# Weight units that stream as the moving operand placed 32 bytes into their slot

## The chip, the cores and the metric

The kernel runs on one core of one Trainium2 chip. The metric is the device time of one execution in microseconds (us). The kernel before takes 2200.12 us, the median of 3 runs (2200.06 to 2201.48).

## What is computed

A small transformer in float32: 256 tokens of width 1024 pass through four layers. Layers 0 and 1 have grouped-query attention (in layer 1 with a sliding window) and layers 2 and 3 a gated delta rule beside dilated attention. The feed-forward part is dense in layers 0, 2 and 3; in layer 1 it is a mixture of 8 experts of which each token uses two:

```
q, k, v = project_qkv(x, w_qkv[i], cos, sin)                 # x @ w, 1024 -> 1536
x = layer_norm(alpha * x + a.reshape(...) @ w_o[i], ...)
swiglu:     (silu(x @ w_gate) * (x @ w_up)) @ w_down         # 1024 -> 3584 -> 1024
moe_swiglu: for e in range(8): out += gates[..., e] * swiglu(x, w_gate[e], w_up[e], w_down[e])
x = x + (p[i] @ w_ple_proj[i]) * sigmoid(x @ w_ple_gate[i])
```

Nearly all the work is activations times weight matrices, and every weight is used once: the weights are streamed from memory.

## The kernel before, in words

**Units.** All weights come as units of 1 MB, [128 partitions x 2048 columns] of float32 (8192 bytes in each partition). SyncE loads them, in the order in which they are used, into `raw`, a ring of 6 slots (L619 in the expert loop, L639 elsewhere). ScalarE copies a unit into a slot of `w_hi`, rounded to the type float32r (`split_hi`, L535), and VectorE writes what the rounding left, `raw - w_hi`, into the same slot of `w_lo` (`split_lo`, L540). `w_hi` and `w_lo` have SPLIT = 3 slots each, one behind another, and unit i lies in slot `place(i)`. The activations are split in the same way into two parts, `xT` and `aT_hi`/`aT_lo`.

**Products.** A product of activations and weights is three float32r matmuls (`mm3`, L829): high by high, high by low, low by high. `nc.tensor.matmul(out, stationary, moving)` first loads its stationary operand, here 128 columns, and then streams the moving one. Weights take one of two roles:

- as the **moving** operand, in pieces of 512 columns, with 128 columns of activations stationary: `part` (the projections qkv, o, the embedding gate, and units 6 to 13 of the input projection of layers 2 and 3), the dense `down`, and all of the experts' `gate_up` and `down`.
- as the **stationary** operand, in pieces of 128 columns, with 256 columns of activations moving: `features` (L897 and L899; the dense gate and up steps but the last two) and `features_in` (through L829; the last two steps, and units 0 to 5 of the input projection). L897 streams the high and the low part of the activations, 256 columns each, in one matmul.

Every piece starts at a multiple of 128 columns in its unit, and every slot and every tensor of activations starts at a multiple of 64 bytes in its partition. The router multiplies by a stationary operand of 8 columns only (`wr_hi`, `wr_lo`), through the same line L829.

**Order.** The order of all the work is written out by hand. Before TensorE reads a unit it waits for VectorE's mark on it (`unit`, L511). ScalarE may overwrite the slot of unit i - 3 with unit i once TensorE has read unit i - 3 for the last time, and SyncE may load unit i + 6 into `raw` once VectorE has split unit i. The experts run in a loop of 8 turns; each turn uses 42 units, 12 matmuls of 512 columns each, and a few transposes (L1160, L1188). A matmul of plain float32 of 512 columns (L816, L824, which keep the engine warm) stands in the trace as two MATMUL instructions.

Of the kernel before, what the change touches and what calls it, by code (L numbers as in the profile page):

```python
# [21 lines left out]
F32R = mybir.dt.float32r  # L22
F32 = mybir.dt.float32
I32 = mybir.dt.int32
ALU = mybir.AluOpType
# [3 lines left out]
P = 128  # L29
# [9 lines left out]
UNIT = 2048  # L39
WARM_START, WARM_LN, WARM_RMS = 4, 2, 4  # L40
RAW = 6
SPLIT = 3
# [188 lines left out]
def build_program(nc, A, plan, debug=None):  # L231
    cst_np, cst_at = constants()
    NC = cst_np.shape[1]
    with ExitStack() as ctx:
        def sb(name, shape, dt=F32):
            return ctx.enter_context(nc.sbuf_tensor(name, shape, dt))


        raw = sb("raw", [P, RAW, UNIT])
        w_hi = sb("w_hi", [P, SPLIT, UNIT], F32R)  # L240
        w_lo = sb("w_lo", [P, SPLIT, UNIT], F32R)
        cst = sb("cst", [P, NC])
        X = sb("X", [P, NT, DM])
        R = sb("R", [P, NT, DM])
# [128 lines left out]
        def events(tag):  # L373
            ev = Events(nc, ctx, plan, tag)

            class E:
                pass
            E.ev = ev
            E.groups = Groups(ev, "groups", 1)
            E.free = [Free(ev, f"free{b}", 1) for b in range(8)]  # L380
            E.dve = ev.new("dve_step")
            E.act = ev.new("act_step")
            E.loaded = [ev.new(f"loaded{s}", 16) for s in range(RAW)]
            E.hi = ev.new("hi_ready")
            E.lo = ev.new("lo_ready")
            E.put = ev.new("ye_stored", 16)
            return E
        M = events("")
# [86 lines left out]
        unit_at, n = {}, 0  # L475
# [9 lines left out]
        after = expert_base + NE * TURN  # L485

        def split_no(i):

            return i - sum(1 for w in whole if w < i)

        def place(i):
            return split_no(i) % SPLIT

        def key_of(i):

            if i >= after and i - after < SPLIT:
                return expert_base + TURN + i - after
            return i
# [8 lines left out]
        def index(key, base=None):  # L507
            return unit_at[key] if base is None else base + order.index(key)
        order = [k for k, _, _ in EXPERT]

        def unit(E, pe, key, base=None):  # L511

            i = index(key, base)
            pe.wait_ge(*E.lo.at("unit", key_of(i)))
            return w_hi[:, place(i), :], w_lo[:, place(i), :]

        def released(E, i, *key):

# [8 lines left out]
        def split_hi(E, ac, i):  # L527

            src = wait_loaded(E, ac, i)
            back = i - SPLIT - (1 if any(i - SPLIT <= w < i for w in whole) else 0)  # L530
            if E is V and i < SPLIT:
                ac.wait_ge(E.groups.sem, 1 + E.ev.turn * plan.per.get("ovf_groups", 0))
            elif back >= 0:
                ac.wait_ge(*reader(E, back))
            nc.scalar.copy(w_hi[:, place(i), :], src).then_inc(*E.hi.mark("unit", i))  # L535

        def split_lo(E, ve, i):

            ve.wait_ge(*E.hi.at("unit", i))
            nc.vector.tensor_tensor(w_lo[:, place(i), :], raw[:, i % RAW, :], w_hi[:, place(i), :].bitcast(F32), ALU.subtract) \  # L540
                .then_inc(*E.lo.mark("unit", i))

        def ahead(E, split, eng, key, base=None):
# [947 lines left out]
        def _(ac):  # L1491
# [3 lines left out]
            def walk(*key):  # L1495
                ahead(M, split_hi, ac, key)
# [390 lines left out]
            for L in range(2):  # L1887
                if L:
                    walk("pg", 0, 3)
                    copy_T((L, "in"), L, 1)  # L1890
                mixer(L)
                want_root()
                if L == 1:
                    ac.wait_ge(*params.at("wr"))
                    nc.scalar.copy(wr_s[0][:, :, :], wr[:, :, :]).then_inc(*M.act.mark("wr"))
                walk("wo", L, 0)
                walk("wo", L, 2)
                norm_root(L, "mix", 0)
                walk("wo", L, 1)
                norm_root(L, "mix", 1)  # L1900
                for t in range(NT):
                    copy_T((L, "mix"), L, t)
                walk("wo", L, 3)
                if L == 0:
                    dense_act(0)
                    want_root()
                    norm_root(L, "ffn", 0)
                    walk("dn", L, FFN_STEPS[L] - 2)
                    walk("dn", L, FFN_STEPS[L] - 1)
                    norm_root(L, "ffn", 1)  # L1910
                    copy_T((L, "ffn"), L, 0)
                    copy_T((L, "ffn"), L, 1)
                else:
                    for i in range(2):
                        split_hi(M, ac, expert_base + i)
                    ac.wait_ge(*M.groups.at("router"))
                    nc.scalar.copy(moe["lgT"][0:NE, :], bank[0][0:NE, 0:S]).then_inc(*M.free[0].mark("router"))
                    for t in range(NT):
                        ac.wait_ge(*x_ready.at(L, "mix", t))
                        ins = nc.scalar.activation(R[:, t, :], X[:, t, :], ACT.Copy, scale=ALPHA)  # L1920
                    ins.then_inc(*M.act.mark("scaled"))
                    ac.wait_ge(*decided.at("m"))
                    nc.scalar.activation(w2, w2, ACT.Exp).then_inc(*M.act.mark("w2"))
                    for i in range(2, SPLIT):
                        split_hi(M, ac, expert_base + i)
                    gathered(M, "moe", "first")
                    nc.scalar.preload_act_table(ACT.Silu)
                    with ac.Fori(0, NE) as e:
                        with ev.loop(e):
                            experts(M, "moe", expert_base)  # L1930
                    ac.wait_ge(*flag_done.at())
                    r = ac.value_load(flag_i[0:1, 0:1], min_val=0, max_val=1)
                    with ac.If(r > 0):
                        with ac.Fori(0, NE) as e:
                            with V.ev.loop(e):
                                experts(V, "ovf", 0)
                        ac.wait_ge(*V.groups.at("ovf", "dn", EXP_STEPS - 1))
                        for i in range(after, after + RAW):
                            ac.wait_ge(*V.loaded[i % RAW].at("again"))
                        for i in range(SPLIT):  # L1940
                            nc.scalar.copy(w_hi[:, place(after + i), :], raw[:, (after + i) % RAW, :]) \
                                .then_inc(*V.hi.mark("again", i))
                    want_root()
                    norm_root(L, "ffn", 0)
                    copy_T((L, "ffn"), L, 0)
                    norm_root(L, "ffn", 1)
                    copy_T((L, "ffn"), L, 1)

                def sigmoid(nb, t):
                    ac.wait_ge(*M.groups.at("pg", L, nb, t))  # L1950
                    nc.scalar.activation(att["sg"][:, 2 * nb + t, :], bank[2 * nb + t][:, :], ACT.Sigmoid) \
                        .then_inc(*M.free[2 * nb + t].mark("pg", L, nb, t))
                sigmoid(0, 0)
                walk("pg", L, 0)
                sigmoid(0, 1)
                walk("pg", L, 1)
                sigmoid(1, 0)
                if L == 0:
                    walk("pg", L, 2)
                    copy_T((1, "in"), 1, 0)  # L1960
                else:
                    want_root()
                    sum_squares(2, "in", 0, x_ready.at(1, "ple", 0))
                    nc.scalar.activation(spare, C("rms_eps"), ACT.Sigmoid)
                sigmoid(1, 1)
# [39 lines left out]
        def _(ve):  # L2005
            V_ = nc.vector
# [12 lines left out]
            def walk(*key):  # L2019
                ahead(M, split_lo, ve, key)  # L2020
# [620 lines left out]
            for L in range(2):  # L2641
# [39 lines left out]
                else:  # L2681
# [14 lines left out]
                    with ve.If(r > 0):  # L2696

                        for n, event in enumerate(V.free + [V.groups]):
                            V_.memset(tick[:, n:n + 1], 0.0).then_inc(event.sem, 1)
                        with ve.Fori(0, NE) as e:  # L2700
                            with V.ev.loop(e):
                                experts(V, "ovf", 0, e, 1)
                        for i in range(SPLIT):
                            u = after + i
                            ve.wait_ge(*V.hi.at("again", i))
                            V_.tensor_tensor(w_lo[:, place(u), :], raw[:, u % RAW, :], w_hi[:, place(u), :].bitcast(F32), ALU.subtract) \
                                .then_inc(*V.lo.mark("again", i))

                    def take_rows(t, nb, total):
# [181 lines left out]
```

## Time and profile before

| | |
|---|---|
| median of 3 runs | 2200.12 us |
| the profiled execution, its own time | 2201.47 us |
| its span, from the first instruction to the last | 2199.7 us |
| TensorE matmuls busy | 2164.4 us (98%), 11360 instructions |
| VectorE busy | 1724.8 us (78%) |
| ScalarE busy | 1416.0 us (64%) |
| mean granted TensorE clock | 0.999 of 2.4 GHz |
| read from memory | 564 MB |

"Busy" is the time in which at least one instruction of the engine was in flight. Matmuls overlap in the pipeline, so the mean duration of one says little about the rate; the rate is the distance between the starts of matmuls that follow one another, or the time of a run of them in the chain of waits divided by their number. The profile names only the tensors that an instruction reads and writes, not the addresses.

### The profile page before, as it was taken

To read this page: it belongs to the slowest core of one execution; us is meant where nothing else is said; L and a number is where in the kernel's file an instruction comes from. 1 tells how busy PE (TensorE), PEld (TensorE's weight loads), DVE (VectorE), ACT (ScalarE), POOL (GpSimd) and SP (SyncE) were. 2 spreads that over 40 slices of the span, in tenths; PEclk is the share of its full clock that TensorE was granted. 3 is DMA by queue.
4 is the path that set the end of the run, shared out by engine and by line. 5 is a ranking of instruction groups with operands and counts; after the bars stand their busy time and mean duration, and the time that the engine had idled before them with its cause. 6 is when DMAs were issued, how large, how long until landed. Compare 5 with 4: busy or idle time off the path is not lost.

```text
span 2199.7 us, 30807 instructions
## 1 busy us (share of the span) xinstructions
PE 2164.4 (98%) x11360; PEld 1806.4 (82%) x11360; DVE 1724.8 (78%) x1976; ACT 1416.0 (64%) x1582; POOL 61.7 (3%) x96
## 2 busy tenths in 40 slices
PE   8999999999999999999999999999999999999998
PEld 6788897778888888888888887779978898988888
DVE  6766556688898888888888889767668886776887
ACT  6644444767777777777777777656566556565554
POOL 3000000020000000000000003000000000000000
PEclk9999999999999999999999999999999999999999
DMA  9755554369999999999999999843135554224451
GB/s 390 273 185 190 192 190 175 120 256 397 358 397 368 390 374 384 378 382 380 371 388 376 389 365 403 323 177 130 68 145 190 184 200 148 86 106 157 188 189 61
DMA packets 83523, 573.26 MB, mean 261 GB/s; under 512 B 9744, under 2 KB 10368, under 8 KB 18224
## 3 DMA queue, kind: packets, MB, share of 16 engines
q1 hardware_dynamic: 77760, 545.29, 65.0%
q0 software_dynamic: 5376, 26.12, 3.2%
q8 instruction: 63, 1.03, 0.2%
q10 hardware_dynamic: 288, 0.52, 0.1%
q14 instruction: 36, 0.29, 0.0%
HBM read 564.03 MB, written 17.83 MB: 265 GB/s over the span
## 4 chain that ended last, share of the span: by engine, by line
PE 87%; DVE 6%; ACT 4%; issue 2%; DMA 1%; SPq 0%; POOL 0%; DVEq 0%; ACTq 0%; POOLq 0%
PE bank L829 64%; PE bank L897 10%; PE bank L899 5%; DVE w_lo L540 1%; ACT w_hi L535 1%; PE bank L1188 1%; DVE arena L2411 1%; PE bank L1316 1%; PE bank L1326 1%; ACT arena L1533 1%; DMA raw<-in_wu_qkv 1%; PE bank L952 0%; DVE arena L2091 0%; PE bank L944 0%; PE bank L798 0%
## 5 line engine op out<-in xcount | busy, mean ns | idle before, releaser
L540 DVE TENSOR_TENSOR w_lo<-raw,w_hi 128x2048 fp32r<-128x2048 f32 x505 | 1156.1, 2300 | 249.4 <-ACT w_hi L535 247.7
L535 ACT CAST w_hi<-raw 128x2048 fp32r<-128x2048 f32 x505 | 964.4, 1912 | 357.5 <-PE bank L829 275.1
L829 PE MATMUL bank<-w_hi,xT 128*128 128x512 f32 x2368 | 751.5, 392 | 6.4 <-DVE w_lo L540 3.3
L829 PEld LDWEIGHTS bank<-w_hi,xT 128*128 128x128 f32 x2368 | 444.6, 188 | 107.6 <-issue 7.0
L829 PE MATMUL bank<-w_lo,xT 128*128 128x512 f32 x1184 | 461.0, 389 | 0.0
L829 PE MATMUL bank<-w_hi,aT_hi 128*128 128x512 f32 x864 | 344.4, 399 | 1.0 <-DVE w_lo L540 1.0
L897 PE MATMUL bank<-xT,w_hi 128*128 128x512 f32 x960 | 339.9, 398 | 1.2 <-DVE xT L2035 0.6
L829 PE MATMUL bank<-w_hi,aT_lo 128*128 128x512 f32 x864 | 337.3, 390 | 0.0
L829 PE MATMUL bank<-w_lo,aT_hi 128*128 128x512 f32 x864 | 336.7, 390 | 0.0
L899 PE MATMUL bank<-xT,w_lo 128*128 128x256 f32 x960 | 269.3, 281 | 0.0
L829 PEld LDWEIGHTS bank<-w_lo,xT 128*128 128x128 f32 x1184 | 222.5, 188 | 44.7 <-issue 0.5
L897 PEld LDWEIGHTS bank<-xT,w_hi 128*128 128x128 f32 x960 | 180.3, 188 | 47.0 <-DVE xT L2035 1.4
L829 PEld LDWEIGHTS bank<-w_hi,aT_hi 128*128 128x128 f32 x864 | 162.3, 188 | 35.6 <-issue 4.0
L829 PEld LDWEIGHTS bank<-w_hi,aT_lo 128*128 128x128 f32 x864 | 162.1, 188 | 35.5
L829 PEld LDWEIGHTS bank<-w_lo,aT_hi 128*128 128x128 f32 x864 | 162.5, 188 | 30.8
L899 PEld LDWEIGHTS bank<-xT,w_lo 128*128 128x128 f32 x960 | 181.2, 189 | 0.9
L829 PE MATMUL bank<-xT,w_hi 128*128 128x256 f32 x768 | 139.0, 283 | 0.0
L829 PEld LDWEIGHTS bank<-xT,w_hi 128*128 128x128 f32 x768 | 120.0, 192 | 0.5
L829 PE MATMUL bank<-xT,w_lo 128*128 128x256 f32 x384 | 108.6, 283 | 0.0
L1688 ACT ACTIVATE arena<-arena,fcw 128x256 f32<-128x256 f32 x72 | 39.4, 595 | 71.4 <-DVE arena L2225 71.4
L829 PEld LDWEIGHTS bank<-xT,w_lo 128*128 128x128 f32 x384 | 73.7, 192 | 0.0
L1648 ACT COPY arena<-bank 128x256 f32<-128x256 f32 x120 | 38.4, 371 | 50.4 <-PE bank L899 50.4
(348 smaller groups left out, 1689.2 us busy)
## 6 DMA issues: line engine op xcount, KB each, us to landing
raw<-in_wu_eg SPq DMA_DIRECT2D x112, 1024.0 KB, 7.3
raw<-in_wu_eu SPq DMA_DIRECT2D x112, 1024.0 KB, 7.2
raw<-in_wu_ed SPq DMA_DIRECT2D x112, 1024.0 KB, 7.2
raw<-in_wu_up SPq DMA_DIRECT2D x44, 1024.0 KB, 4.8
raw<-in_wu_ffn_gu SPq DMA_DIRECT2D x28, 1024.0 KB, 4.8
raw<-in_wu_in SPq DMA_DIRECT2D x28, 1024.0 KB, 4.8
raw<-in_wu_down SPq DMA_DIRECT2D x22, 1024.0 KB, 4.8
raw<-in_wu_ffn_d SPq DMA_DIRECT2D x14, 1024.0 KB, 4.8
```

What stands on the lines that cost most here:

```text
L535: nc.scalar.copy(w_hi[:, place(i), :], src).then_inc(*E.hi.mark("unit", i))
L540: nc.vector.tensor_tensor(w_lo[:, place(i), :], raw[:, i % RAW, :], w_hi[:, place(i), :].bitcast(F32), ALU.subtract) \
L829: mm = nc.tensor.matmul(o, l[i], r[j], start=(first and n == 0), stop=(last and n == 2), skip_group_check=not lone)
L897: nc.tensor.matmul(both, u[0][:, c0:c0 + P], x_both[:, :, kc, :], start=(kc == 0), stop=False, skip_group_check=True)
L899: mm = nc.tensor.matmul(o[:, S:2 * S], u[1][:, c0:c0 + P], xT[0][:, kc, :], start=False, stop=(kc == KC - 1), skip_group_check=True)
L1188: mm = nc.tensor.transpose(o[:, c * P:(c + 1) * P], moe["h"][:, f % 2, c * P:(c + 1) * P], ident)
L1316: of_level(n, "X", t, t, lambda dst, i: nc.tensor.matmul(dst, dn["LT"][:, i, :], dn["D"][:, i, :], start=True, stop=True))
L1326: of_level(n, "D", t, 2 + t, lambda dst, i: nc.tensor.matmul(dst, dn["DT"][:, i, :], dn["Xl"][:, i, :], start=True, stop=True))
L1533: ins = nc.scalar.activation(att["pr"][:, i, e, cols], att["s"][:, i, e, cols], ACT.Exp, bias=nmax[:, i, e, q:q + 1], scale=-1.0, accum_ou ...
L1648: ins = nc.scalar.copy(ffn["cor"][:, half, m, :], bank[4 + 2 * half + m][:, S:2 * S])
L1688: ins = nc.scalar.activation(buf[:, s % 2, m, :], src, ACT.Identity, bias=fcw[:, c, 3:4], scale=fcw[:, c, 2:3])
L2411: ins = V_.scalar_tensor_tensor(dn["cv"][:, c, d:S], bank[b][:, m * S:m * S + S - d], cw[:, L - 2, c, tap:tap + 1], dn["cv"][:, c, d:S], A ...
```

## The change

Each slot of `w_hi` and `w_lo` becomes 32 columns (128 bytes) longer, 8320 bytes instead of 8192. A unit whose matmuls use it as the moving operand stands 8 columns (32 bytes) behind the start of its slot; a unit that is used as the stationary operand starts where the slot starts. ScalarE, VectorE and TensorE take the place from one new function, `split_at`. No instruction is added, removed or moved in any engine's order, no wait changes, and every instruction handles as many elements as before. The tensors that are allocated behind the two (`cst`, `X`, `R`, `xT`, `aT` and the rest) start 768 bytes later.

```diff
         raw = sb("raw", [P, RAW, UNIT])
-        w_hi = sb("w_hi", [P, SPLIT, UNIT], F32R)
-        w_lo = sb("w_lo", [P, SPLIT, UNIT], F32R)
+        MOVING_AT = 8
+        w_room = [sb(f"w_{part}", [P, SPLIT, UNIT + 32], F32R) for part in ("hi", "lo")]
+        w_hi, w_lo = [w[:, :, MOVING_AT:MOVING_AT + UNIT] for w in w_room]
...
+        stationary = {i for key, i in unit_at.items() if (key[0] == "gu" or (key[0] == "in" and key[2] < 6))}
+
+        def split_at(E, i):
+
+            at = 0 if E is M and i in stationary else MOVING_AT
+            return [w[:, place(i), at:at + UNIT] for w in w_room]
...
             pe.wait_ge(*E.lo.at("unit", key_of(i)))
-            return w_hi[:, place(i), :], w_lo[:, place(i), :]
+            return split_at(E, i)
...
-            nc.scalar.copy(w_hi[:, place(i), :], src).then_inc(*E.hi.mark("unit", i))
+            nc.scalar.copy(split_at(E, i)[0], src).then_inc(*E.hi.mark("unit", i))
...
-            nc.vector.tensor_tensor(w_lo[:, place(i), :], raw[:, i % RAW, :], w_hi[:, place(i), :].bitcast(F32), ALU.subtract) \
+            hi, lo = split_at(E, i)
+            nc.vector.tensor_tensor(lo, raw[:, i % RAW, :], hi.bitcast(F32), ALU.subtract) \
```

The expert units are not in `unit_at`, so they all count as moving. The two other places that split units (for an overflow of the experts, a branch that this input does not take) are changed alike.

## Rows read from the trace of the kernel before

**Rows 1.** The page: busy time by engine, then the chain by engine and line.
```profile
PE 2164.4 (98%) x11360; PEld 1806.4 (82%) x11360; DVE 1724.8 (78%) x1976; ACT 1416.0 (64%) x1582; POOL 61.7 (3%) x96
...
PE 87%; DVE 6%; ACT 4%; issue 2%; DMA 1%; SPq 0%; POOL 0%; DVEq 0%; ACTq 0%; POOLq 0%
```

**Rows 2.** Groups of TensorE's instructions by shape; xcount, busy and mean, idle before.
```profile
L829 PE MATMUL bank<-w_hi,xT 128*128 128x512 f32 x2368 | 751.5, 392 | 6.4 <-DVE w_lo L540 3.3 <-DVE w_lo L2604 2.1 <-DVE xT L2035 0.7
L829 PE MATMUL bank<-w_lo,xT 128*128 128x512 f32 x1184 | 461.0, 389 | 0.0
L829 PE MATMUL bank<-w_hi,aT_hi 128*128 128x512 f32 x864 | 344.4, 399 | 1.0 <-DVE w_lo L540 1.0
...
L829 PE MATMUL bank<-w_hi,aT_lo 128*128 128x512 f32 x864 | 337.3, 390 | 0.0
L829 PE MATMUL bank<-w_lo,aT_hi 128*128 128x512 f32 x864 | 336.7, 390 | 0.0
```

**Rows 3.** Chain of waits, 600 to 700 us: start, length in us, what.
```profile
619.35 16.35 PE bank L829 x72
```

**Rows 4.** Timeline of TensorE, 296 to 302 us: weights stationary, 256 columns moving.
```profile
296.23 0.28 PE L829 MATMUL bank<-xT,w_lo 128*128 128x256 f32 x1
...
299.11 0.28 PE L829 MATMUL bank<-xT,w_lo 128*128 128x256 f32 x1
```

**Rows 5.** Timeline of TensorE, 452 to 455.6 us: the router, 8 stationary columns.
```profile
452.65 0.40 PE L829 MATMUL bank<-xT,wr_hi 128*8 128x256 f32 x2 [0.47 <-DVE xT L2032]
...
455.10 0.40 PE L829 MATMUL bank<-xT,wr_hi 128*8 128x256 f32 x2
```

**Rows 6.** Timeline of TensorE, 2001.5 to 2006 us: matmuls of plain float32.
```profile
2001.89 3.60 PE L816 MATMUL bank<-cst 128*128 128x512 f32 x8
2005.33 0.93 PE L798 MATMUL bank<-R,X 128*128 128x128 f32 x6
```

**Rows 7.** Chain of waits, 200 to 240 us: gate and up of the dense layer.
```profile
209.66 0.23 PE bank L897
...
220.61 5.50 PE bank L829 x24
```

**Rows 8.** Timeline of TensorE, 237 to 239 us: from gate and up to down.
```profile
237.24 0.40 PE L829 MATMUL bank<-w_hi,aT_hi 128*128 128x512 f32 x1
...
238.87 0.39 PE L829 MATMUL bank<-w_lo,aT_hi 128*128 128x512 f32 x1
```

**Rows 9.** Busy time in the expert loop: us, engines with counts, PEclk, DMA share, GB/s.
```profile
505.00:1435.00 930.00, 924.04 (x4182) 758.42 (x4180) 817.79 (x460) 689.76 (x470) 19.26 (x8) 1.00 0.97 377
```

**Rows 10.** Waits by total, 520 to 1400 us.
```profile
ACT w_hi L535 <- PE bank L829: 176.7, 252, 2.2
DVE w_lo L540 <- ACT w_hi L535: 100.9, 190, 1.5
```

**Rows 11.** DMA, 600 to 1300 us: GB/s in 40 slices; one unit's landing.
```profile
GB/s 406 414 366 382 370 361 350 424 404 370 368 361 385 358 411 383 389 367 379 355 394 384 402 372 382 371 352 405 381 400 387 367 375 338 415 400 378 386 362 363
...
raw<-in_wu_eg SPq DMA_DIRECT2D x82, 1024.0 KB, 7.3
```

**Rows 12.** Groups of ScalarE and VectorE by shape.
```profile
L535 ACT CAST w_hi<-raw 128x2048 fp32r<-128x2048 f32 x505 | 964.4, 1912 | 357.5 <-PE bank L829 275.1 <-PE bank L899 80.1 <-DMA raw<-in_wu_qkv 2.0
...
L540 DVE TENSOR_TENSOR w_lo<-raw,w_hi 128x2048 fp32r<-128x2048 f32 x505 | 1156.1, 2300 | 249.4 <-ACT w_hi L535 247.7
...
L2264 DVE SCALAR_TENSOR_TENSOR arena<-arena,fcw 128x255 f32<-128x255 f32 x72 | 31.7, 481 | 44.3 <-ACT arena L1688 44.3
...
L2159 DVE SCALAR_TENSOR_TENSOR X<-R,small,vec 128x1024 f32<-128x1024 f32 x8 | 10.3, 1285 | 0.3
```

More of the change, by code:

```diff
@@ L1940, in _ @@
                         for i in range(SPLIT):
-                            nc.scalar.copy(w_hi[:, place(after + i), :], raw[:, (after + i) % RAW, :]) \
+                            nc.scalar.copy(split_at(M, after + i)[0], raw[:, (after + i) % RAW, :]) \
                                 .then_inc(*V.hi.mark("again", i))
@@ L2705, in _ @@
                             ve.wait_ge(*V.hi.at("again", i))
-                            V_.tensor_tensor(w_lo[:, place(u), :], raw[:, u % RAW, :], w_hi[:, place(u), :].bitcast(F32), ALU.subtract) \
+                            hi, lo = split_at(M, u)
+                            V_.tensor_tensor(lo, raw[:, u % RAW, :], hi.bitcast(F32), ALU.subtract) \
                                 .then_inc(*V.lo.mark("again", i))
```

## The prediction, made before the changed kernel had run

> **What bounds the kernel now.** I read the page first. TensorE is busy for 2164.4 of 2199.7 us, and 87% of the chain that ended last is its own matmuls [rows 1]. The groups by shape say which: 2368 + 1184 + 3 x 864 = 6144 matmuls of 512 columns stream weights, and before the largest group the engine sat idle for only 6.4 us in the whole run [rows 2]. So TensorE seldom waits for a unit, and the question is its rate. The mean durations (389 to 399 ns) are those of a pipeline; the chain of waits gives the rate: a run of 72 such matmuls takes 16.35 us, 227.1 ns each [rows 3]. The granted clock there is 1.00 of 2.4 GHz [rows 9], at which 512 columns at one per cycle are 213.3 ns. Each matmul costs 13.8 ns more than its columns.
>
> I then looked for what that excess depends on.
> - Weights stationary, 256 columns moving: from 296.23 to 299.11 us stand eight groups of three, so 24 starts in 2.88 us, 120.0 ns each [rows 4]. 256 columns are 106.7 ns: excess 13.3 ns, the same for half the columns. It is a price per matmul, not per byte.
> - The router, only 8 stationary columns: seven groups of three from 452.65 to 455.10 us, 116.7 ns each [rows 5]. Excess 10.0 ns. With almost nothing to load into the array 3.3 ns go, 10 stay.
> - Plain float32: 8 instructions from 2001.89 to 2005.33 us, 430 ns each [rows 6]. That is two cycles per column (426.7 ns) and an excess of 3.3 ns, with the same load of 128 columns. The moving operand is read at half the rate there.
> - Gate and up, where one matmul streams two runs of 256 columns and the next one run: 31 pairs from 209.66 to 220.61 us, 353.2 ns a pair [rows 7]. Less 120.0 for the single run, the one with two runs takes 233.2 ns, 6.1 more than one run of 512.
> - Just behind such pairs the same down matmuls that later run at 227.1 start 1.63 us / 7 = 232.9 ns apart [rows 8]. So the excess is not a constant of the instruction: it depends on how the streams stood to one another before.
>
> My reading: when float32r is streamed at a column per cycle, reading the moving operand and loading the next stationary operand get in one another's way a little, and the phase between them matters. In the kernel before every operand of both kinds starts at a multiple of 64 bytes, so the trace shows a single setting of that phase. The change gives it another one, for 6144 of the matmuls.
>
> **The change, part by part.** *TensorE, weights moving.* 6144 matmuls, at an unknown change of price. From below, the most that can go is the excess down to that of plain float32, 13.8 - 3.3 = 10.5 ns: 6144 x 10.5 = 64.5 us. From above, the worst rate in these rows is that of a stream that starts a second run, +6.1 ns: 6144 x 6.1 = 37.5 us lost. Zero lies between. I take the nearest row in which the load is practically absent and all else is as before, the router's: 120.0 - 116.7 = 3.3 ns off each, 6144 x 3.3 = 20.3 us. That is the part of the excess which two streams out of each other's way would save; the other 10 ns stay in a row without a load, and nothing shows that an offset moves them.
>
> *TensorE, weights stationary.* These units keep their place and the activations that they meet stay at multiples of 64 bytes; only distances of 128 bytes and more change between tensors. I count 0, with 3.3 ns on some of them either way as the bound: the two shapes of L897 and L899 alone are 1920 matmuls, 6 us.
>
> *ScalarE and VectorE.* They write and read 32 bytes further on. 505 casts of 1912 ns and 505 subtractions of 2300 ns [rows 12]. The convolution (L2264) works on 255 columns that start one element into a row: 481 ns; the aligned L2159 takes 1285 ns for 1024 columns. At 1.042 ns a column that leaves 215 and 218 ns fixed: an odd start costs VectorE nothing visible. I count 0 for both. Even 50 ns on each would be covered: ScalarE waits 176.7 us and VectorE 100.9 us for others in the expert loop [rows 10].
>
> *What the gain triggers.* A unit is 12 matmuls, 2.73 us; a slot must be refilled within two units, 5.45 us, and needs 1.91 + 2.30 = 4.2 us. With 3.3 ns off each the window is 5.37 us, with 10.5 off 5.20: still enough. VectorE is busy for 817.8 of 930 us there (88%) [rows 9]; at the full gain that becomes 92%. The DMA moves 377 GB/s [rows 9]; the full gain asks for 377 x 227.1 / 216.6 = 395, and slices of the same stretch reach 424 [rows 11]. A transfer lands 7.3 us after its issue, out of six units, 16.4 us, less the 4.2 of the split. So neither takes the gain away, and as the runs of matmuls are themselves the path, all of it counts.
>
> *Sum.* The profiled execution's own time is 2201.5 us; less 20.3 is 2181.2. The median of the runs lies 1.3 us lower, so the forecast is 2179.8, say 2180 us.
>
> **What the pages say.** Two rules of the Trainium skill speak against this. "SBUF — State Buffer", section "Specifications (TRN2)", has lines of 16 bytes as the unit in which an operand is read; 32 bytes are two such lines, the operand starts on a line as before and touches as many, and by that rule the time stays at 2200. No row here can show it, as nothing of float32r starts elsewhere than at a multiple of 64 bytes. And "TensorE: Matmul & The Clock Gate", section "Step-by-step: what each phase is for", gives the moving operand and the weight load ports of their own, so that a load steals nothing from a running matmul. By that rule too nothing would change; the router's row disagrees in part, with 3.3 ns less when the load is small.
>
> **The rivals.**
> - *Nothing changes: 2200 us.* The excess is a fixed price of a float32r matmul. For it: it is 13.8 and 13.3 ns for 512 and 256 columns, as a fixed price would be, and the router's smaller one may come from the shorter load itself. In the kernel `turn_probs` transposes stationary data that start at odd elements, beside aligned transposes elsewhere, and nothing in TensorE's groups sets them apart. Against it: rows 8, where the same matmul has two prices.
> - *The whole excess goes.* The offset lets the two reads alternate without a meeting, and what is left is plain float32's 3.3 ns: 2200 - 64.5 = 2136 us. For it: that row has the same load. Against it: the router keeps 10 ns without one.
> - *Slower, on the far side of zero.* A run of 2048 bytes that begins 32 bytes into a 64-byte stretch ends in one more such stretch (33 instead of 32). If the reader fetches in stretches of 64 bytes, each matmul pays for a start in mid-stretch as L897 pays for its second run, 6.1 ns: 2200 + 37.5 = 2238 us. It decides from the first nanosecond, since nothing hides TensorE. For it: rows 7, a second start does cost. Against it: L897's second run lies 8 KB away, not next door.
> - *The change does less than it says.* All units of the experts and of `part` go through `split_at`, so 6144 matmuls are reached; I see no way in which only some would be.
>
> **How the numbers follow.** Forecast (a few ns off each moving matmul) 0.38; whole excess 0.15; nothing 0.26; slower 0.21. A measurement of this kernel tells a change from none at about 0.2%, 4.4 us. Faster 0.53, same 0.26, slower 0.21. The forecast's own range is 1.5 to 7 ns, 2157 to 2191 us. For 8 in 10 the range needs no change (2200), most of the whole excess (down to 2135) and the milder half of the slower case (up to 3 ns, 2219): 2135 to 2219 us.
>
> **What would show it right or wrong.** Right: in the expert loop a run of 72 matmuls in the chain takes 16.35 - 72 x 0.0033 = 16.11 us; the loop is shorter by 4032 x 3.3 ns = 13 us; the pairs of L897 and L899 stay at 353 ns and the 256-column matmuls with stationary weights at 120; L535 and L540 keep 1912 and 2300 ns. If the run takes 15.6 us the whole excess went; if 16.35, nothing; if about 16.8, the offset costs a start. The forecast's mechanism would be wrong if the stationary matmuls move as much as the moving ones, or if ScalarE's or VectorE's durations carry the difference, or if TensorE begins to wait for L540 in the expert loop by more than a few us.

## The result, and the profile after

The changed kernel takes 2229.41 us (median of 4 runs, 2229.19 to 2229.84), beside 2200.3 us for the kernel before (4 runs, 2200.06 to 2201.48). The ratio is 1.0129, with a 95% interval of 1.0116 to 1.0143: 29 us slower, where 20 us faster was forecast. 2229 also lies above the range of 2135 to 2219 us.

The page, line 1 and the first line of the chain, to be read beside [rows 1]:

```profile
PE 2195.4 (99%) x11360; PEld 1807.6 (81%) x11360; DVE 1726.1 (77%) x1976; ACT 1413.6 (63%) x1582; POOL 63.5 (3%) x96
...
PE 91%; DVE 4%; ACT 2%; issue 1%; DMA 1%; SPq 0%; POOL 0%; DVEq 0%; ACTq 0%; POOLq 0%
```

TensorE is busy 31.0 us longer in a span that is 28.3 us longer (2228.0 against 2199.7 us). VectorE's and ScalarE's busy time moved by 1.3 and 2.4 us. So the time went into TensorE's own work, and the next view shows into which instructions. These are its groups by shape (count, busy us, mean ns, idle before), beside [rows 2]; all lines of the kernel now stand 8 lower, L829 is L837, L897 and L899 are L905 and L907:

```profile
L837 PE MATMUL bank<-w_hi,xT 128*128 128x512 f32 x2368 | 762.9, 397 | 4.4 <-DVE w_lo L548 3.4 <-DVE xT L2043 0.7
L837 PE MATMUL bank<-w_lo,xT 128*128 128x512 f32 x1184 | 467.8, 395 | 0.0
L837 PE MATMUL bank<-w_hi,aT_hi 128*128 128x512 f32 x864 | 346.8, 401 | 1.0 <-DVE w_lo L548 1.0
L837 PE MATMUL bank<-w_hi,aT_lo 128*128 128x512 f32 x864 | 342.4, 396 | 0.0
L837 PE MATMUL bank<-w_lo,aT_hi 128*128 128x512 f32 x864 | 340.9, 395 | 0.0
L905 PE MATMUL bank<-xT,w_hi 128*128 128x512 f32 x960 | 338.7, 395 | 1.1 <-DVE xT L2043 0.6 <-issue 0.4
L907 PE MATMUL bank<-xT,w_lo 128*128 128x256 f32 x960 | 269.3, 281 | 0.0
```

The five groups with weights moving, 6144 matmuls, were busy for 2230.9 us and are now busy for 2260.8: +29.9, the whole loss. (Matmuls of different groups overlap in the pipeline, so these sums are larger than the engine's busy time.) The two groups with weights stationary, 339.9 and 269.3 us before, are at 338.7 and 269.3. Idle time in front of the first group fell, from 6.4 to 4.4 us: nobody waits more. (The distances from each start to the next, summed over the trace, give the same picture: +28.9 us for the five groups, -1.3 us for the pairs.)

The chain of waits in the expert loop (start, length in us, what), beside the 16.35 us of [rows 3]:

```profile
624.33 0.44 PE bank L1196 x4
624.77 16.79 PE bank L837 x72
641.56 0.44 PE bank L1196 x4
641.99 16.78 PE bank L837 x72
```

16.79 us are 233.2 ns each instead of 227.1. The transposes between two runs keep their 0.44 us. It holds for every run: of 30 such runs between 520 and 1430 us one takes 17.05 us and 29 take 16.78 or 16.79; in the kernel before one took 16.63 and 28 of 29 took 16.35. One turn of the loop was 118.65 us and is 121.42, which is 2.77 us for 504 matmuls, 5.5 ns each, and 22 us for eight turns. The other 7 us come from the 2112 moving matmuls outside it, where a run of 24 went from the 5.50 us of [rows 7] to 5.61 us.

A closer look at the steady part of one run, in the timeline of TensorE (start, length; the xN at the end of a line tells how many are grouped). The kernel before:

```profile
629.64 0.39 PE L829 MATMUL bank<-w_lo,xT 128*128 128x512 f32 x1
629.87 0.62 PE L829 MATMUL bank<-w_hi,xT 128*128 128x512 f32 x2
...
634.40 0.39 PE L829 MATMUL bank<-w_lo,xT 128*128 128x512 f32 x1
```

and the changed one:

```profile
634.64 0.40 PE L837 MATMUL bank<-w_lo,xT 128*128 128x512 f32 x1
634.87 0.63 PE L837 MATMUL bank<-w_hi,xT 128*128 128x512 f32 x2
...
639.53 0.40 PE L837 MATMUL bank<-w_lo,xT 128*128 128x512 f32 x1
```

Seven groups of three lie between first and last: 21 starts in 4.76 us, 226.7 ns each, before; 21 in 4.89 us, 232.9 ns each, after. At the full clock of 2.4 GHz 226.67 ns are 544 cycles and 233.33 ns are 560. The kernel before needs some eight to ten matmuls behind every interruption, of 224 to 236 ns each, until it runs at 544; that is [rows 8], seen from nearer. The changed kernel never gets there. So it loses 6.2 ns only on the matmuls behind this run-in, and 4.7 ns on the average over all 6144.

What could have carried the loss instead, and doesn't: the granted clock in the loop (the third number from the end), 1.00 as in [rows 9]:

```profile
505.00:1450.00 945.00, 940.47 (x4168) 757.37 (x4168) 815.70 (x449) 686.96 (x466) 21.19 (x8) 1.00 0.96 369
```

the waits of the two splits by total (us, times, longest), beside [rows 10]:

```profile
ACT w_hi L542 <- PE bank L837: 190.9, 247, 2.1
DVE w_lo L548 <- ACT w_hi L542: 115.9, 191, 1.5
```

and the splits themselves, ScalarE's and VectorE's groups by shape beside [rows 12]:

```profile
L542 ACT CAST w_hi<-raw 128x2048 fp32r<-128x2048 f32 x505 | 961.9, 1907 | 380.7 <-PE bank L837 296.9 <-PE bank L907 81.2 <-DMA raw<-in_wu_qkv 2.6
```

```profile
L548 DVE TENSOR_TENSOR w_lo<-raw,w_hi 128x2048 fp32r<-128x2048 f32 x505 | 1157.4, 2300 | 273.4 <-ACT w_hi L542 271.6
```

The casts take 1907 ns (1912 before), the subtractions 2300 as before, 32 bytes further on. ScalarE waits longer for TensorE, and VectorE for ScalarE; TensorE doesn't wait longer for them. The memory traffic fell from 377 to 369 GB/s, which is what the longer turn alone gives (377 x 118.65 / 121.42 = 368).

### The profile page after: what moved, and what is told of

It reads as the page before. It is cut to its first block, busy times and chain, and to the rows that moved or that the text cites. A ratio compares the mean times of both kernels' runs of the same rounds, so it can differ in the third digit from the quotient of the medians.

```text
span 2228.0 us, 30807 instructions
## 1 busy us (share of the span) xinstructions
PE 2195.4 (99%) x11360; PEld 1807.6 (81%) x11360; DVE 1726.1 (77%) x1976; ACT 1413.6 (63%) x1582; POOL 63.5 (3%) x96
## 4 chain that ended last, share of the span: by engine, by line
PE 91%; DVE 4%; ACT 2%; issue 1%; DMA 1%; SPq 0%; POOL 0%; DVEq 0%; ACTq 0%; POOLq 0%
PE bank L837 67%; PE bank L905 10%; PE bank L907 5%; PE bank L1196 1%; DVE w_lo L548 1%; PE bank L1324 1%; PE bank L1334 1%; ACT arena L1541 1%; DMA raw<-in_wu_qkv 1%; DVE arena L2099 0%; PE bank L960 0%; ACT w_hi L542 0%; DVE arena L2419 0%; PE bank L952 0%; PE bank L806 0%
## 5 line engine op out<-in xcount | busy, mean ns | idle before, releaser
L542 ACT CAST w_hi<-raw 128x2048 fp32r<-128x2048 f32 x505 | 961.9, 1907 | 380.7 <-PE bank L837 296.9
L837 PE MATMUL bank<-w_hi,xT 128*128 128x512 f32 x2368 | 762.9, 397 | 4.4 <-DVE w_lo L548 3.4
L837 PEld LDWEIGHTS bank<-w_hi,xT 128*128 128x128 f32 x2368 | 444.4, 188 | 115.6 <-DVE w_lo L548 5.4
L837 PE MATMUL bank<-w_lo,xT 128*128 128x512 f32 x1184 | 467.8, 395 | 0.0
L837 PE MATMUL bank<-w_hi,aT_hi 128*128 128x512 f32 x864 | 346.8, 401 | 1.0 <-DVE w_lo L548 1.0
L837 PE MATMUL bank<-w_hi,aT_lo 128*128 128x512 f32 x864 | 342.4, 396 | 0.0
L837 PE MATMUL bank<-w_lo,aT_hi 128*128 128x512 f32 x864 | 340.9, 395 | 0.0
L905 PE MATMUL bank<-xT,w_hi 128*128 128x512 f32 x960 | 338.7, 395 | 1.1 <-DVE xT L2043 0.6
L907 PE MATMUL bank<-xT,w_lo 128*128 128x256 f32 x960 | 269.3, 281 | 0.0
L837 PEld LDWEIGHTS bank<-w_lo,xT 128*128 128x128 f32 x1184 | 222.5, 188 | 53.3 <-issue 0.5
L905 PEld LDWEIGHTS bank<-xT,w_hi 128*128 128x128 f32 x960 | 180.2, 188 | 45.6 <-DVE xT L2043 1.4
L837 PEld LDWEIGHTS bank<-w_hi,aT_hi 128*128 128x128 f32 x864 | 162.0, 187 | 39.8 <-issue 4.0
L837 PEld LDWEIGHTS bank<-w_hi,aT_lo 128*128 128x128 f32 x864 | 162.4, 188 | 37.4
L837 PEld LDWEIGHTS bank<-w_lo,aT_hi 128*128 128x128 f32 x864 | 162.6, 188 | 35.9
L907 PEld LDWEIGHTS bank<-xT,w_lo 128*128 128x128 f32 x960 | 180.7, 188 | 1.2
L837 PE MATMUL bank<-xT,w_hi 128*128 128x256 f32 x768 | 139.3, 284 | 0.0
L837 PEld LDWEIGHTS bank<-xT,w_hi 128*128 128x128 f32 x768 | 119.6, 191 | 0.6
L837 PE MATMUL bank<-xT,w_lo 128*128 128x256 f32 x384 | 108.8, 283 | 0.0
L837 PEld LDWEIGHTS bank<-xT,w_lo 128*128 128x128 f32 x384 | 73.3, 191 | 0.0
```

What stands on the lines that cost most here:

```text
L542: nc.scalar.copy(split_at(E, i)[0], src).then_inc(*E.hi.mark("unit", i))
L837: mm = nc.tensor.matmul(o, l[i], r[j], start=(first and n == 0), stop=(last and n == 2), skip_group_check=not lone)
L905: nc.tensor.matmul(both, u[0][:, c0:c0 + P], x_both[:, :, kc, :], start=(kc == 0), stop=False, skip_group_check=True)
L907: mm = nc.tensor.matmul(o[:, S:2 * S], u[1][:, c0:c0 + P], xT[0][:, kc, :], start=False, stop=(kc == KC - 1), skip_group_check=True)
```

## The experiments

What the trace of after leaves open is which of the things that moved costs these 6.2 ns. The edit does more than its words say: moving operands start 32 bytes further on; slots are 128 bytes longer, so that the slots of `w_hi` no longer all start at the same place modulo 256 bytes, nor do those of `w_lo`; and `xT` and `aT` stand 768 bytes further on. In the kernel before, the starts of `w_hi`, `w_lo`, `xT`, `aT_hi` and `aT_lo` all leave the same remainder modulo 512 bytes. (This is worked out from the sizes of the tensors: all between them are multiples of 512 bytes but `cst`, whose 3560 bytes are taken to be rounded up to 3584. No view shows addresses.) For a moving operand and the stationary one with which it is multiplied or which is loaded next to it, this means: **their distance is a multiple of 256 bytes, everywhere**. In the changed kernel it is 32 or 160 bytes modulo 256, by slot and part.

Four theories: (A) the start 32 bytes into a stretch of 64 costs, the prediction's slower case; (B) what costs are the changed distances of 128 bytes and more that the longer slots bring; (C) the offset of 32 bytes between the two operands costs, whichever of them is moved; (D), formed behind the first four runs, the distance modulo 256 bytes decides, 128 included. Where a kernel ran once, its time stands beside one run of the kernel before on the same chip; the nine runs of the kernel before on one chip lay between 2200.17 and 2204.33 us, so a difference of less than about 4 us between two single runs shows nothing by itself.

**Longer slots, no offset.**

```diff
-        MOVING_AT = 8
+        MOVING_AT = 0
```

> The changed kernel with the offset at 0: the slots stay 128 bytes longer and the tensors behind stay 768 bytes later, but all weights start at their slot's start. Theory A (the start 32 bytes into a 64-byte stretch is what costs): about 2200 us, runs of 72 expert matmuls in 16.35 us as before. Theory B (distances of 128 bytes and more between the weights and the activations matter): about 2229 us, runs in 16.8 us. Theory C (the offset between the two operands of a matmul, modulo 64 bytes): about 2200 us.

Measured: 2219.01 us, beside 2201.69: +17.3 us. The chain of waits, expert loop:

```profile
621.73 16.64 PE bank L837 x72
638.37 0.44 PE bank L1196 x4
638.81 16.65 PE bank L837 x72
```

16.64 / 72 = 231.1 ns. So a part of the loss needs no 32 bytes at all, and theories A and C, which gave 2200 us here, can't be all of it. The prediction had put such distances ("128 bytes and more") down at nothing.

**All weights 32 bytes further on, activations not.** To the kernel before, 8 columns of padding ahead of `w_hi` and 120 behind `w_lo`, so that everything behind keeps its place modulo 512 bytes:

```diff
         raw = sb("raw", [P, RAW, UNIT])
+        sb("pad_a", [P, 8])
         w_hi = sb("w_hi", [P, SPLIT, UNIT], F32R)
         w_lo = sb("w_lo", [P, SPLIT, UNIT], F32R)
+        sb("pad_b", [P, 120])
```

> The kernel before with 32 bytes of room ahead of w_hi and 480 behind w_lo: all weights, stationary ones too, stand 32 bytes further on, nothing else moves against another modulo 512 bytes. Theories A and C: about 2229 us or, if the stationary units suffer or gain too, up to 10 us to either side. Theory B: 2200 us.

Measured: 2226.95 us, beside 2201.69: +25.3 us. Chain, then two groups by shape:

```profile
623.35 16.80 PE bank L831 x72
```

```profile
L831 PE MATMUL bank<-w_hi,xT 128*128 128x512 f32 x2368 | 763.7, 397 | 3.7 <-DVE w_lo L542 2.7 <-DVE xT L2037 0.7
...
L899 PE MATMUL bank<-xT,w_hi 128*128 128x512 f32 x960 | 336.3, 394 | 1.1 <-DVE xT L2037 0.6 <-issue 0.4
```

Theory B alone gave 2200 us here. The run of 72 takes what it takes in the changed kernel, with slots of the old length. And the pairs of gate and up, in which the weights are stationary, became a little cheaper: 336.3 us against 339.9, 349.1 ns a pair from start to start instead of 353.2.

**Everything 32 bytes further on.** Only `pad_a`:

```diff
         raw = sb("raw", [P, RAW, UNIT])
+        sb("pad_a", [P, 8])
         w_hi = sb("w_hi", [P, SPLIT, UNIT], F32R)
```

> The kernel before with 32 bytes of room ahead of w_hi and none behind: weights and activations all start 32 bytes into a 64-byte stretch, their distances are those of before. Theory A: slower than the changed kernel, since the 3072 matmuls with moving activations pay too: 2200 + (6144 + 3072) x 4.7 ns = 2243 us. Theories B and C: 2200 us.

Measured: 2201.92 us, beside 2201.69. Chain:

```profile
617.35 16.35 PE bank L830 x72
```

The weights and the activations all start 32 bytes into a stretch of 64, and nothing is lost, where theory A gave 2243 us. Theory A falls: where a stream starts is of no account by itself.

**Activations 32 bytes further on, weights not.** `pad_a` of 8 columns ahead of `xT`, 120 columns behind `aT_lo`:

```diff
+        sb("pad_a", [P, 8])
         x_both = sb("xT", [P, 2, KC, S], F32R)
         xT = [x_both[:, part, :, :] for part in range(2)]
         aT = [sb(f"aT_{part}", [P, KC, S], F32R) for part in ("hi", "lo")]
+        sb("pad_b", [P, 120])
```

> The kernel before with 32 bytes of room ahead of xT and 480 behind aT_lo: the activations stand 32 bytes further on, the weights keep their place. Theory A: the 6144 matmuls with moving weights as before, the 3072 with moving activations 4.7 ns more: 2214 us. Theory C: the offset between the operands is 32 bytes in both kinds, so about 2229 us or more. Theory B: 2200 us.

Measured: 2227.76 us, beside 2201.69: +26.1 us. Chain:

```profile
622.83 16.81 PE bank L831 x72
```

The weights stand exactly as in the kernel before, and the loss is there. It belongs to the distance between the two operands.

**The price by distance.** A kernel of its own, which computes nothing of the reference: 48 settings, each 48 equal float32r matmuls back to back on data that don't change, with the starts of both operands given in bytes, two short plain float32 matmuls between settings:

```
for c, (n, w, m, s) in enumerate(CONFIGS):   # moving columns, stationary columns, starts in bytes
    ...
    for i in range(48):
        matmul(o[0:w, 0:n], sta[:, s//4 : s//4 + w], mov[:, m//4 : m//4 + n])
```

> A kernel of its own that computes nothing of the reference: it repeats one float32r matmul 48 times for each of 48 settings (moving columns, stationary columns, start of the moving and of the stationary operand), with two plain float32 matmuls ahead of each. Theory C, sharpened by the first runs (what counts is the distance between the start addresses of the moving operand and of the stationary operand that is loaded meanwhile): at 512 moving and 128 stationary columns a distance of 0 gives 226.7 ns between starts, 32 bytes gives 233.3, and both operands 32 bytes on gives 226.7 again; with 8 stationary columns the distance makes no difference. Rival (the distance only picks one of several patterns that what came before leaves possible): settings of one distance differ between repeats of the run, and 0 and 32 bytes come out alike when one matmul is simply repeated.

Measured, in the chain of waits (one row a setting), 512 columns moving and 128 stationary. In their order here: moving operand at 0, 4, 32, 64 and 256 bytes; stationary one at 32; both at 32:

```profile
19.01 10.96 PE bank L64 x48
30.37 11.40 PE bank L64 x48
...
77.01 11.24 PE bank L64 x48
...
111.93 11.05 PE bank L64 x48
...
181.61 10.97 PE bank L64 x48
...
296.65 11.22 PE bank L64 x48
...
354.59 10.95 PE bank L64 x48
```

Each row holds a run-in, as the runs of the kernel do; the mean of the last 24 distances from start to start gives the steady price in ns:

| moving minus stationary start, bytes | 512 columns |
|---|---|
| 0, 256, 512, 1024 | 226.7 |
| 4 | 236.7 |
| 16 | 231.7 |
| 8, 24, 32, 40, 48 | 233.3 |
| 64 | 228.9 |
| 96, 192, 224, 288 | 233.3 |
| 128 | 232.7 |
| 160 | 234.2 |
| both moved by 32 or by 64 | 226.7 |

The table repeats after 256 bytes (0 and 256 agree, 32 and 288, 64 and 320), and a stationary operand moved by d costs, within 0.6 ns, what a moving one moved by -d does: 96 bytes on the one and 160 on the other are both 234.2 ns. The kernel's own numbers are in it: 226.7 before; 233 after, with distances of 32 and 160; and between them the kernel with longer slots alone, where half of the streams stand at 0 and half at 128. Theory D is the only one of the four with room for all of these; C alone has none for the loss at 128. Its prices are not met exactly where distances alternate: half at 226.7 and half at 232.7 would be 229.7 ns, and with longer slots alone most stretches of twelve matmuls behind the run-in take 230 to 233. No distance is below 226.7: **the kernel before already had the cheapest setting for its 6144 moving matmuls.**

With 256 columns moving the order is another one: 120.0 ns at 0, 116.7 at 32, 117.8 at 64. With 8 stationary columns 512 columns take 226.7 ns at 0 and 231.7 at 32, where no difference was expected: the price isn't one of loading 128 columns. With 32 stationary columns it is the other way round, 231.7 ns at 0 and 226.7 at 32, and with 64 there is hardly a difference (230.0 and 230.8). So the table holds for 128 stationary columns.

**The shapes with weights stationary.** The same kernel, 46 other settings; "pair" is L897's two runs of 256 columns followed by L899's one:

> A kernel of its own that computes nothing of the reference, like the first one, now for the shapes of gate and up: a matmul of two runs of 256 columns followed by one of 256, and 256 columns alone, each with the stationary operand moved by 0 to 240 bytes; and more distances at 512 columns. Theory D (the distance of the two start addresses modulo 256 bytes decides): at 512 columns nothing below 226.7 ns; both operands 4 or 8 bytes on, which keeps the distance at 0, gives 226.7 too; pairs take 353 ns at distance 0 and 349 to 350 at 32 bytes, as in the whole kernels. Rival (alignment of each operand to its own 32 or 64 bytes matters as well): both operands 4 or 8 bytes on are slower than 226.7.

Measured, steady, the stationary operand moved: a pair takes 353.3 ns at 0 as in [rows 7], 346.7 at 16, 48, 96 and 224 bytes, 353.3 again at 32, 64 and 192, and 350 to 351 at 128, 160 and 208. 256 columns alone take 120.0 ns at 0 as in [rows 4], and 113.3 at 64 bytes, the lowest (106.7 would be one column a cycle). The chain, at 0 and at 64 bytes:

```profile
143.97 5.80 PE bank L68 x48
...
168.53 5.49 PE bank L68 x48
```

One of the whole kernels agrees with this. With the activations alone 32 bytes further on, which for weights that are stationary is a moving start 32 bytes on, the pairs ran at 346.7 ns and the single 256 columns at 116.7, as the two kernels of equal matmuls have them.

The measurement of shapes also shows a limit of theory D, on the side of its rival: with both operands at 4 bytes 512 columns take 237.8 ns, with both at 8 bytes 231.1, both at 16 bytes 231.1 (in the run before), both at 128 bytes 226.7. Off the multiples of 32 bytes the place of each counts as well, not only their distance: with the moving operand at 4 bytes the price is 236.5 to 237.8 ns wherever the stationary one was put (0, 4, 8, 16 or 32). And not every odd distance costs: the moving operand at 252 bytes takes 226.7 ns too, at 12 bytes 228.9, at 80 and 112 bytes 231.1, at 144, 176 and 240 bytes 233.3, at 208 bytes 234.7.

Back in the kernel, three runs with slots that are 256 bytes longer, so that all slots of a role stand alike.

**Slots 256 bytes longer, no offset.**

```diff
-        MOVING_AT = 8
-        w_room = [sb(f"w_{part}", [P, SPLIT, UNIT + 32], F32R) for part in ("hi", "lo")]
+        MOVING_AT = 0
+        w_room = [sb(f"w_{part}", [P, SPLIT, UNIT + 64], F32R) for part in ("hi", "lo")]
```

> The changed kernel with slots 64 columns (256 bytes) longer in place of 32 and the offset at 0. Theory D: all distances are those of the kernel before modulo 256 bytes, so 2200 us, against 2219 with slots 128 bytes longer. Rival (distances modulo 512 or more count): near 2219.

Measured: 2199.55 us, beside 2199.46; the run of 72 takes 16.35 us. Longer slots cost nothing when they are longer by 256 bytes: the 17 us of the first experiment came from the 128.

**Slots 256 bytes longer, moving units at 32 bytes.** As the one above, but `MOVING_AT = 8`:

> The changed kernel, offset of 32 bytes and all, with slots 256 bytes longer in place of 128. Theory D: 233.3 ns for each of the 6144 matmuls, of which about 227.5 in the kernel before, so 2200 + 6144 x 5.8 ns = 2236 at most; by the run with all weights 32 bytes on (2227, with the stationary units about 6 us faster than here) 2233 us. Rival (the changed kernel's loss is the sum of a loss by the longer slots, 17 us, and one by the offset, 12 us): 2212 us.

Measured: 2234.15 us, beside 2199.46: +34.7 us. The five moving groups are busy for 2261.9 us (31.0 more), and a run of 72 takes 16.80 us. The offset that the change is named for is enough, without any help from the slots, for the whole loss. The two effects don't add: 17 and 35 would be 52. The moving matmuls cost nearly the same as in the change (2260.8 us there). Of the 4.3 us between the two spans (2232.3 and 2228.0), 1.1 lie in the moving matmuls by their starts, 2.0 in the pairs and 1.1 in the single 256 columns: with slots 128 bytes longer the stationary units also met other distances, and ran at 350 to 352 ns a pair instead of 353.

**The offset on the other role.** Moving units at 0, stationary ones at 32 bytes:

```diff
-            at = 0 if E is M and i in stationary else MOVING_AT
+            at = STATIONARY_AT if E is M and i in stationary else MOVING_AT    # 8; MOVING_AT = 0
```

> The change the other way round: slots 256 bytes longer, moving units at their slot's start, stationary units 32 bytes into it. Theory D: moving ones as before; 960 pairs at 349.1 instead of 353.2 ns and 1152 matmuls of 256 columns at 117 to 119 instead of 120.4: 3.9 + 1.8 to 3.9 us less, 2193 to 2195 us. Rival (the gain seen on stationary units with all weights 32 bytes on came from neighbours): 2200.

Measured: 2199.39 us, beside 2199.46: none of the 6 to 8 us that were expected. The moving runs are back at 16.35 us. The pairs are where they were in [rows 7], as the measurement of shapes says for 32 bytes; chain of waits:

```profile
207.76 0.24 PE bank L905
208.00 0.12 PE bank L907
208.12 0.23 PE bank L905
208.35 0.12 PE bank L907
208.46 0.24 PE bank L905
208.70 0.12 PE bank L907
208.82 0.23 PE bank L905
```

Three pairs from 207.76 to 208.82 us, 353 ns each. I had read the cheaper pairs of "weights 32 bytes further on" as a price of that distance, and it was not so. Cut into stretches of six pairs, that trace has 88 at 347 ns and 33 at 353, and this one 116 at 353, at the same distance of 32 bytes. What picked the one rate there and the other here is not shown.

**Each role at its own place.** Moving units at 0; the units of `features`, which run as pairs, at 224 bytes; the others that are stationary, which run as single 256 columns, at 64 bytes:

```diff
-        MOVING_AT = 8
-        w_room = [sb(f"w_{part}", [P, SPLIT, UNIT + 32], F32R) for part in ("hi", "lo")]
+        MOVING_AT, PAIR_AT, SINGLE_AT = 0, 56, 16
+        w_room = [sb(f"w_{part}", [P, SPLIT, UNIT + 64], F32R) for part in ("hi", "lo")]
...
-            at = 0 if E is M and i in stationary else MOVING_AT
+            at = stationary.get(i, MOVING_AT) if E is M else MOVING_AT    # unit -> PAIR_AT or SINGLE_AT
```

> Slots 256 bytes longer; moving units at their slot's start; stationary units of the steps that alternate two runs and one run of 256 columns 224 bytes into it, the other stationary units (256 columns alone) 64 bytes. By the second kernel of its own: pairs 346.7 instead of 353.3 ns, 960 of them, 6.4 us less; 1152 matmuls at 113.3 instead of 120.0 ns, 7.7 us less; moving ones as before. Theory D with the prices carried over: 2200 - 14 = 2186 us. Rival (what a matmul pays follows the pattern that the stream happens to settle in, as in the reverse kernel, where half of the pairs kept a 240 ns matmul): between 2190 and 2200.

Measured, 5 runs: 2192.44 us (2191.94 to 2194.2), beside 2201.19 (9 runs): ratio 0.9960, interval 0.9946 to 0.9973. It beats the kernel before by 0.4% and the changed one by more. The expected 2186 us were missed, and the time lies in the range of the rival, 2190 to 2200. Chain of waits, pairs, and a run of moving weights:

```profile
207.37 0.12 PE bank L908
...
208.41 0.12 PE bank L908
...
209.45 0.12 PE bank L908
...
614.92 16.35 PE bank L838 x72
```

Between two of the first three rows lie three pairs: 1.04 us, 346.7 ns a pair. The start-to-start sums fall by 5.2 us for the pairs and by 4.1 us for the 256 columns alone; the latter less than 113.3 ns each would give, since most of them run at 118 (52 of 74 stretches of twelve). **With the pairs at 96 bytes** (`PAIR_AT` 24 instead of 56):

> As the kernel before this one, but 96 bytes for the units of the pairs; the same 346.7 ns in the kernel of its own. Theory D: the same time within 1 us, 2186. Rival (the pattern settled in differs): the pairs' share of the gain, 6.4 us, is partly or wholly lost, up to 2193.

Measured, 5 runs: 2193.39 us (2192.96 to 2195.32), ratio 0.9962, interval 0.9948 to 0.9975. The two can't be told apart, as the equal prices of 96 and 224 bytes say.

**Does it matter what came before?** [Rows 8] had shown one matmul at two prices. The last kernel starts 12 settings behind 0, 1, 2 and 10 matmuls of 512 columns at distance 0:

> A kernel of its own that computes nothing of the reference: the patterns of the second one at four distances each, every one started four ways, behind 0, 1, 2 or 10 matmuls of 512 columns at distance 0. Theory D in its strict form (the distance alone sets the rate): the four starts of a setting end at the same rate. Rival (for some distances the stream can settle in several patterns, and what ran before picks one): the four starts of the stationary-weight patterns at 32 or 96 bytes end at different rates, for instance 346.7 and 353.3 ns a pair, while 512 columns at distance 0 always end at 226.7.

Measured: 512 columns settle at 226.7 ns (distance 0), 233.3 (32 and 224) and 232 to 233 (128) whatever came before. Among the others, two settings don't keep one rate: the pair at distance 0 takes 346.7 ns behind no such matmul and 353.3 behind 1, 2 or 10; 256 columns at 64 bytes take 113.3 ns behind 0, 1 or 2 and 117.8 behind 10. Chain of waits, the pair at distance 0, behind none (upper three rows) and behind one (lower three):

```profile
222.54 0.23 PE bank L67
...
222.89 0.23 PE bank L67
...
223.24 0.23 PE bank L67
...
229.90 0.24 PE bank L67
...
230.96 0.24 PE bank L67
...
232.01 0.24 PE bank L67
```

The upper rows are neighbours, one pair apart, 0.35 us; the lower ones are three pairs apart, 1.06 us. In the measurement of shapes the same pair, also behind no such matmul, had taken 353.3 ns; but it came first there and sixteen settings later here. So for a few settings there are two lasting rates, and the history picks one; what in the history does so is not shown. For the shape that decides here there is one.

## Why the prediction was wrong

- **The step that failed is the price of a moving matmul.** The text took "the nearest row in which the load is practically absent and all else is as before, the router's", 3.3 ns off each. Two things were wrong in it. The router's row has 256 columns, and the term was for 512: at 512 columns 8 stationary columns instead of 128 give 226.7 ns at distance 0, nothing less (measurement of distances). And a row with a small load says what is saved without the load, not what is saved when it comes at another moment. In place of -3.3 ns the steady price rose by 6.2 (by 6.6 in the measurement, at 32 bytes), and by 4.7 on the average over 6144, +28.9 us instead of -20.3.
- **What was not asked: how good is the present setting among all?** "The trace shows a single setting" was right, though by luck: starts at multiples of 64 bytes would leave four distances modulo 256, and only because all were multiples of 256 was there one. From one setting nothing tells whether it is a good one. At distance 0 the shape stands at the minimum of all that were measured. The excess over the columns, 13.4 ns in the steady part and 13.8 with the run-in, is what the best setting leaves. The bound from below, plain float32's 3.3 ns, was not reached by float32r in any setting: the least excess is 6.6 ns, with 256 columns at 113.3.
- **The term for the stationary units was small for a wrong reason.** The measured pairs moved by -1.3 us, inside the 6 us allowed. But "only distances of 128 bytes and more change" was counted as nothing, and such a distance alone costs the moving matmuls 17 us (longer slots, no offset). The slots' length was seen and not priced for them.
- **The slower rival had the size and the wrong mechanism.** It forecast about 16.8 us for the run of 72 and 2238 us; 16.79 and 2229 were measured. But its start in mid-stretch is refuted: with everything 32 bytes further on the time is 2201.92 us, and with the activations alone moved, the weights where they were, it is 2227.76. Its price, 6.1 ns, was taken from L897's second run, and that it came near the 6.6 is not explained by anything shown here.
- **What was right.** That the excess depends on how the two operands stand to one another; moving either operand alone costs 25 and 26 us, moving both costs nothing. That nothing hides TensorE's rate: the loss in the matmuls is the loss in the time. That ScalarE and VectorE don't feel the 32 bytes (1907 and 2300 ns). That all 6144 matmuls are reached. And that the pairs and the single 256 columns stay near 353 and 120 ns.
- **The two rules from the pages.** By the Trainium skill, "SBUF — State Buffer", section "Specifications (TRN2)", with lines of 16 bytes, 32 bytes more should have changed nothing. The measured time disagrees, 2229 against 2200 us, and the prices at 0, 64 and 96 bytes (226.7, 228.9 and 233.3 ns) differ though all are whole lines. The skill's "TensorE: Matmul & The Clock Gate", section "Step-by-step: what each phase is for", has separate ports for the two operands, by which a load steals no reading from a running matmul. Here the price of a matmul depends on the distance of the two starts, 226.7 to 236.7 ns, so where the load reads is not without effect on the stream. Whether the two share a read, or anything else, is not shown by any run.

Left open: why the pattern repeats after 256 bytes and has these values; whether the distance that counts is that to the matmul's own stationary operand or to the next one, which is loaded meanwhile (all matmuls of a setting had the same); what makes two rates last in some settings; and why the kernel with the offset on the other role did not end earlier, although its single 256 columns ran at 118.3 ns in the steady part as measured for 32 bytes.

## What to carry to other kernels

Where float32r matmuls with 512 moving and 128 stationary columns set the time, keep the start of the moving and of the stationary operand at a distance of a multiple of 256 bytes in their partition, at multiples of 32 bytes each, and look at this whenever padding or a new tensor shifts what lies behind it. Before an offset is tried in a kernel, measure its price for the very shape (columns, runs, what is stationary) in a kernel of equal matmuls, the present setting included: 48 prices came from one run, and the version that gained (0.9960) was read off such a table. A row of another shape is no price for this one, and an excess over the ideal is no gain until some setting has been seen below it.

## What the runs showed of the hardware that was not expected

- The rate of float32r matmuls depends on the distance of their operands' starts, at multiples of 32 bytes modulo 256: at 512 moving and 128 stationary columns 226.7 ns at 0, 228.9 at 64, 232.7 at 128, 233.3 at 32, 234.2 at 160; and 236.7 at 4, but 226.7 at 252. It does so with 8 stationary columns too (226.7 and 231.7 ns at 0 and 32), and with 32 in the opposite sense (231.7 and 226.7).
- Other shapes have their minimum elsewhere, with the stationary operand moved: 256 columns 113.3 ns at 64 bytes (120.0 at 0), two runs of 256 and one of 256 346.7 ns at 16, 48, 96 or 224 bytes (353.3 at 0).
- Behind an interruption the stream at distance 0 takes some eight to ten matmuls, of 224 to 236 ns each, to come to 226.7; and two settings have two lasting rates (346.7 or 353.3 ns; 113.3 or 117.8 ns), chosen by what ran before them.
